# Normalising each head pair's output: eight one-column sums and transposes replaced by two full-width sums of squares

## The reference

```python
q = heads(jax.nn.silu(q_raw)) * (HGRN_KDIM ** -0.5)
v = heads(i_raw)
k_f, g_f = _hgrn2_forget(ffwd_raw, lb_fwd)
k_b, g_b = _hgrn2_forget(fbwd_raw, lb_bwd)
o_fwd = _gla_chunked(q, heads(k_f), v, heads(g_f))
o_bwd = flip(_gla_chunked(flip(q), flip(heads(k_b)), flip(v), flip(heads(g_b))))
o = (o_fwd + o_bwd).transpose(0, 2, 1, 3)
o = _rmsnorm(o, gnorm_w).reshape(b, s, HGRN_HEADS * HGRN_VDIM)
return o * jax.nn.silu(g_raw)
```

## Time and profile before

| what | value |
|---|---|
| median of 3 runs | 1879.22 us (1875.61 to 1879.58) |
| profiled execution's own time | 1879.22 us |
| its span in the profile | 1877.4 us |
| PE busy | 1680.7 us, 90% of the span |
| DVE, ACT, POOL busy | 780.7, 626.0, 551.4 us |
| mean granted PE clock | 0.948 of full speed |
| DMA | 123.5 MB, 66 GB/s on average |
| the head stage with attention, pairs 1 to 3 | about 123 to 478 us |
| the gates stage, with the attention of the fourth pair | about 478 to 683 us |

### The profile page before, as it was taken

One profiled execution on the slowest core, in us unless ns is written; L12 is line 12 of the kernel. 1 busy time (PEld: TensorE's weight loads), 2 busy tenths in 40 slices (PEclk: granted clock), 3 DMA queues, 4 the chain that ended last, 5 costly groups with the idle time before them and its releaser, 6 DMA issues.

```text
span 1877.4 us, 22957 instructions
## 1 busy us (share of the span) xinstructions
PE 1680.7 (90%) x9317; PEld 1308.7 (70%) x9317; DVE 780.7 (42%) x1229; ACT 626.0 (33%) x1011; POOL 551.4 (29%) x287
## 2 busy tenths in 40 slices
PE   5999999999689889999877999899996888999996
PEld 2788988889578667777646898555684665555564
DVE  3336365363765321111147611666514445444422
ACT  4322312313212321222332132666513224455632
POOL 2431213112433343333424222333423321010220
PEclk8999999899879989999888999899998889999998
DMA  4242212213123335343211112000011020000101
GB/s 135 92 145 68 90 45 67 89 35 99 50 63 90 90 112 179 112 134 123 90 45 45 63 57 68 18 18 18 1 59 45 23 72 17 17 18 23 45 23 45
DMA packets 128929, 123.50 MB, mean 66 GB/s; under 512 B 11252, under 2 KB 125040, under 8 KB 128848
## 3 DMA queue, kind: packets, MB, share of 16 engines
q1 hardware_dynamic: 128848, 122.37, 20.8%
HBM read 117.91 MB, written 2.10 MB: 64 GB/s over the span
## 4 chain that ended last, share of the span: by engine, by line
PE 63%; issue 13%; DVE 12%; POOL 7%; ACT 3%; DMA 2%; SPq 0%; DVEq 0%; POOLq 0%; ACTq 0%
PE ps L1801 5%; PE ps L1755 5%; PE ps L1756 5%; PE ps L1757 5%; POOL w_lo L982 4%; PE ps L2159 3%; PE ps L1959 3%; PE ps L2138 3%; PE ps L1960 3%; PE ps L1961 3%; PE ps L2148 3%; PE ps L1923 2%; PE ps L2025 2%; DMA raw<-in_w_in_dram 2%; PE ps L2016 2%
## 5 line engine op out<-in xcount | busy, mean ns | idle before, releaser
L982 POOL TENSOR_TENSOR w_lo<-raw,w_hi 128x2048 fp32r<-128x2048 f32 (+2 forms) x86 | 372.4, 4331 | 778.4 <-ACT w_hi L591 699.9
L1755 PE MATMUL ps<-h_hi,w_hi 128*128 128x512 f32 x656 | 274.1, 418 | 41.4 <-POOL h_lo L1042 14.0
L1756 PE MATMUL ps<-h_lo,w_hi 128*128 128x512 f32 x656 | 265.6, 405 | 0.0
L1757 PE MATMUL ps<-h_hi,w_lo 128*128 128x512 f32 x656 | 264.7, 404 | 0.0
L591 ACT ACTIVATE w_hi<-raw 128x2048 fp32r<-128x2048 f32 (+1 forms) x78 | 147.4, 1890 | 332.9 <-DMA raw<-in_w_in_dram 111.0
L1755 PEld LDWEIGHTS ps<-h_hi,w_hi 128*128 128x128 f32 x656 | 129.2, 197 | 82.2 <-issue 34.5
L1757 PEld LDWEIGHTS ps<-h_hi,w_lo 128*128 128x128 f32 x656 | 129.1, 197 | 29.1
L1756 PEld LDWEIGHTS ps<-h_lo,w_hi 128*128 128x128 f32 x656 | 129.4, 197 | 24.9
L1801 PE MATMUL ps<-qf,kf 128*128 128x64 f32 x448 | 91.0, 286 | 31.4 <-DVE tot_b L1241 27.8
L1801 PEld LDWEIGHTS ps<-qf,kf 128*128 128x128 f32 x448 | 73.2, 203 | 35.8 <-DVE tot_b L1241 29.9
L1801 PE MATMUL ps<-qb,kb 128*128 128x64 f32 x448 | 91.5, 288 | 0.0
(11 more groups left out here) (347 smaller groups left out, 3538.3 us busy)
## 6 DMA issues: line engine op xcount, KB each, us to landing
raw<-in_w_in_dram SPq DMA_DIRECT2D x32, 1024.0 KB
raw<-in_ada_w_dram SPq DMA_DIRECT2D x24, 1024.0 KB
raw<-in_a_w_in_dram SPq DMA_DIRECT2D x10, 1024.0 KB
raw<-in_w_in_dram SPq DMA_DIRECT2D x16, 512.0 KB
raw<-in_b_w_in_dram SPq DMA_DIRECT2D x5, 1024.0 KB
raw<-in_w_proj_a_dram SPq DMA_DIRECT2D x4, 1024.0 KB
raw<-in_w_proj_b_dram SPq DMA_DIRECT2D x4, 1024.0 KB
raw<-in_w_out_dram SPq DMA_DIRECT2D x4, 1024.0 KB
```

The lines of the kernel that those rows point to most:

```text
L982: nc.gpsimd.tensor_tensor(w_lo[:, ph.w(s), c], raw[:, s % 2, c], w_hi[:, ph.w(s), c].bitcast(F32), ALU.subtract).then_inc(s_lo, 1)
L1755: mm(ps[:, j, :], wh[:, k, c], xh[:, k, :], start=(k == 0), stop=False)
L1756: mm(ps[:, j, :], wh[:, k, c], xl[:, k, :], start=False, stop=False)
L1757: last = mm(ps[:, j, :], wl[:, k, c], xh[:, k, :], start=False, stop=(k == KT - 1))
```

## The change

The sums of squares are no longer taken per token on the partitions. Step 11 becomes two matmuls with a 128x128 matrix of ones as weights, one for each head, whose result [128, 512] holds each token's sum on every partition already. The scaling, the reciprocal and the root then work on the full [128, 1024] instead of [128, 8]; the copy that spread the root and step 12, the transposes, go away. `gla_out` goes away too: its two multiplications stand at the end of `gla_norm`, in slot 10, and the gate is kept in a tile of its own, `g_a`, instead of `y_a`. PE has 12 steps in place of 13, so all waits on `s_gla` are renumbered.

```diff
+        g_a = at("g_a", [P, 2, S], F32, r_s + 4 * KB)
...
-        g_ms = at("g_ms", [P, 2, 2 * NT], F32, region(64))
...
                 if tt == 10:
                     act.wait_ge(s_gms, g + 1)
-                    nc.scalar.activation(g_ms[:, 0, :], g_ms[:, 1, :], ACT.Sqrt).then_inc(s_grs, 1)
-                    act.wait_ge(s_grs, 2 * g + 1)
-                    nc.scalar.activation(qb[:, :, :].rearrange("p h (n c) -> p (h n) c", c=P),
-                                         g_ms[:, 0, :].unsqueeze(2).to_broadcast([P, 2 * NT, P]), ACT.Copy).then_inc(s_grs, 1)
+                    nc.scalar.activation(qb[:, :, :], kf[:, :, :], ACT.Sqrt).then_inc(s_grs, 1)
...
             def gla_norm(g):
-                dve.wait_ge(s_gla, 13 * g + 12)
-                v.tensor_scalar(g_ms[:, 0, :], ps[:, 4, 0:2 * NT], 1.0 / P, RMS_EPS, ALU.mult, ALU.add).then_inc(s_gcp_dve, 1)
+                dve.wait_ge(s_gla, 12 * g + 12)
+                v.tensor_scalar(kb[:, :, :], ps[:, 4:6, :], 1.0 / P, RMS_EPS, ALU.mult, ALU.add).then_inc(s_gcp_dve, 1)
                 dve.wait_ge(s_gcp_dve, 9 * g + 8)
-                v.reciprocal(g_ms[:, 1, :], g_ms[:, 0, :]).then_inc(s_gms, 1)
-
-            def gla_out(g):
-                dve.wait_ge(s_gla, 13 * g + 13)
-                gate = y_a[:, bass.ds(2 * g, 2), :]
-                v.scalar_tensor_tensor(kb[:, :, :], ps[:, 4:6, :], cols("gnorm_w"), gate, ALU.mult, ALU.mult).then_inc(s_gcp_dve, 1)
+                v.reciprocal(kf[:, :, :], kb[:, :, :]).then_inc(s_gms, 1)
+                dve.wait_ge(s_grs, g + 1)
+                v.scalar_tensor_tensor(kb[:, :, :], ps[:, 2:4, :], cols("gnorm_w"), qb[:, :, :],
+                                       ALU.mult, ALU.mult).then_inc(s_gcp_dve, 1)
                 dve.wait_ge(s_gcp_dve, 9 * g + 9)
-                v.tensor_tensor(gate, ps[:, 2:4, :], kb[:, :, :], ALU.mult).then_inc(s_y, 1)
+                v.tensor_tensor(y_a[:, bass.ds(2 * g, 2), :], kb[:, :, :], g_a[:, :, :], ALU.mult).then_inc(s_y, 1)
                 dve.wait_ge(s_y, g + 2)
...
                             if tt == 10:
                                 gla_norm(g)
-                            if tt == 11:
-                                gla_out(g)
...
-                            v.tensor_tensor(y_a[:, bass.ds(2 * it + j, 1), :], bank, a, ALU.mult).then_inc(s_free, 1)
+                            v.tensor_tensor(g_a[:, j, :], bank, a, ALU.mult).then_inc(s_free, 1)
...
-                elif step == 11:
+                else:
                     pe.wait_ge(s_osq, g + 1)
                     for h in range(2):
-                        for n in range(NT):
-                            last = mm(ps[:, 4, NT * h + n:NT * h + n + 1], qf[:, h, n * P:(n + 1) * P], ones[:, 0:1], start=True, stop=True)
-                else:
-                    pe.wait_ge(s_grs, 2 * g + 2)
-                    for h in range(2):
-                        for n in range(NT):
-                            last = nc.tensor.transpose(ps[:, 4 + h, n * P:(n + 1) * P], qb[:, h, n * P:(n + 1) * P], ident[:, :])
+                        last = mm(ps[:, 4 + h, :], ones[:, :], qf[:, h, :], start=True, stop=True)
                 last.then_inc(s_gla, 1)
```

More of the change, by code:

```diff
@@ L662, in gla_act @@
                     nc.scalar.activation(kb[:, :, :], kb_new[:, :, :], ACT.Copy).then_inc(s_kcopy, 1)
-                    act.wait_ge(s_gla, 13 * g + 1)
+                    act.wait_ge(s_gla, 12 * g + 1)
                     nc.scalar.activation(a_diag[:, :, :, :].rearrange("p h n s -> p (h n s)"),
@@ L666, in gla_act @@
                 if tt == 7:
-                    act.wait_ge(s_gla, 13 * g + 9)
+                    act.wait_ge(s_gla, 12 * g + 9)
                     nc.scalar.activation(a_128[:, :, :, :].rearrange("p h n s -> p (h n s)"),
@@ L670, in gla_act @@
                 if tt == 8:
-                    act.wait_ge(s_gla, 13 * g + 10)
+                    act.wait_ge(s_gla, 12 * g + 10)
                     nc.scalar.activation(a_256[:, :, :, :].rearrange("p h n s -> p (h n s)"),
@@ L674, in gla_act @@
                 if tt == 9:
-                    act.wait_ge(s_gla, 13 * g + 11)
+                    act.wait_ge(s_gla, 12 * g + 11)
                     nc.scalar.activation(qf[:, :, :], ps[:, 2:4, :], ACT.Square).then_inc(s_osq, 1)
@@ L1229, in gla_double @@
                     dve.wait_ge(s_gcp_act, 3 * g + 1)
-                dve.wait_ge(s_gla, 13 * g + l + 1)
+                dve.wait_ge(s_gla, 12 * g + l + 1)
                 if l > 1:
@@ L1277, in head_tiles @@
                                 gla_init(g)
-                                dve.wait_ge(s_gla, 13 * g + 1)
+                                dve.wait_ge(s_gla, 12 * g + 1)
                             if tt <= 7:
@@ L1283, in head_tiles @@
                             if tt == 8:
-                                dve.wait_ge(s_gla, 13 * g + 11)
+                                dve.wait_ge(s_gla, 12 * g + 11)
                             if tt == 10:
                                 gla_norm(g)
-                            if tt == 11:
-                                gla_out(g)
                         bank, a, b = ps[:, j, :], tmp[:, 2 * j, :], tmp[:, 2 * j + 1, :]
@@ L1855, in head_tiles @@
                                 gla(it - 1, 0)
-                            gla(it - 1, tt + 1)
+                            if tt <= 10:
+                                gla(it - 1, tt + 1)
                         if j == 0 and s in (4, 7):
@@ L1879, in _ @@
                         gla(PAIRS - 1, 0)
-                    if tt <= 11:
+                    if tt <= 10:
                         gla(PAIRS - 1, tt + 1)
```

## The result

| | before | changed |
|---|---|---|
| median (5 runs each) | 1878.70 us (1875.32 to 1879.58) | 1889.59 us (1886.45 to 1890.86) |
| ratio | 1 | 1.0063, 95% interval 1.0045 to 1.0082 |
| profiled execution, own time / span | 1879.22 / 1877.4 us | 1891.38 / 1889.5 us |
| PE, DVE busy | 1680.7, 780.7 us | 1677.2, 813.4 us |
| mean granted clock | 0.948 | 0.946 |

The changed kernel is 10.9 us slower by the medians; 10.1 was forecast (1889.3 us, range 1883 to 1898).

What follows compares the result with a forecast made beforehand. PE was taken to bound the head stage (busy 111.3 of 112.5 us), so its delays count. Terms 9.3 + 0.95 + 4.2 - 3.5 - 0.85 = +10.1 us on 1879.22 gave 1889.3 us, range 1883 to 1898.

Steps and rivals of the forecast that it cites:

- DVE's chain: At a pair's end, scaling through both products precedes the first `ga` tile's read-out; tile free after 12.4 us.
- Ends of pairs 1 and 2: Projection starts 5.9 us later, the 1.29 us wait for `qb` disappears; step 1 +4.65 us, twice, 9.3 us.
- End of pair 3: Step 0 waits for the output, 0.25 us later, and DVE has one more tile to read out: +0.95 us.
- Fourth pair: In the gates stage, DVE's longer chain delays the end of POOL's `w_lo`: +4.2 us.
- let it through in full: Fourth pair's `w_lo` delay counted whole, since SP's next load and PE's group 6 projection wait for it; bounds 0 and 5.
- The clock: Granted clock around the pair ends: -3.5 us for ends of pairs 1 and 2, -0.85 for the dip behind step 11.
- The dip behind step 11 of pair 2: Clock of 0.83 over ten us behind one-column matmuls, 1.7 us lost; half counted as regained, -0.85 us.
- 3 (POOL holds the reciprocal): POOL's `w_lo` makes the reciprocal wait, starting 3.4 us later at ends of pairs 1 to 3: +10.2, 1899.5 us; chance 0.03.
- 4 (a fast reciprocal): The wide reciprocal takes 1.22 us, like DVE's other operations: -5.6, 1873.6 us; chance 0.04.
- 5 (taken up later): Fourth pair's delay vanishes in the load waits and the clock gives all back: +1.75, 1881 us; chance 0.05.
- 1 (1897): PE's new idle costs 1.65 us twice and the old clock falls still come: +17.8, 1897 us; chance 0.12.
- 2 (1885.2): The clock gives all back, with no loss behind the idle time: +5.95, 1885.2 us; chance 0.16.

Runs made afterwards that it cites:

- e1: The changed kernel with DVE's reciprocal of 1024 columns cut to 8, so its output is not the reference's: 1866.97 us, ratio 0.9936.
- e6: The kernel before with only ACT's `w_hi` moved behind the copies of `kf` and `kb`: 1864.75 us, ratio 0.9939.
- e9: The changed kernel with reciprocal and root replaced by one ACT pass, an inverse square root: 1865.9 us, ratio 0.9945.
- e11: The kernel before with the wide normalisation for the fourth pair alone, in the gates stage: 1880.2 us, ratio 1.0031.
- e7: The changed kernel run and profiled once more, unaltered: 1887.63 us, ratio 1.0072.

## Why the prediction was right

Right in sign and size, and by its own steps; that the sum came within 1 us is in part luck, since chance falls of the clock move a profile by 3 us and two terms were mis-sized in opposite directions. Figures are from the first profile of the changed kernel.

- **DVE's chain.** Forecast: reciprocal 6.55, root 1.06, the projection 12.5 us after DVE's start, behind 6.9 us of idle. Measured: 6.55, 1.06, 12.46 (224.54 to 237.00), 6.61. The terms as listed, with 0.3 of hand-overs, add up to 12.55 to the free tile and not to the 12.4 that was written; the pauses turned out shorter, and the slip cost nothing. The line through 512 and 768 columns held at 1024, and `e1` shows that this term is the loss.
- **Ends of pairs 1 and 2.** Forecast: the delays without the clock are +9.3 us. Measured: over both cycles PE's time without work went from 4.9 to 15.6 us and its work at full clock from 225.0 (`e6`) to 223.5 (`e9`): +9.2. `qb` was indeed held up (5.63 us), and nobody waited for it.
- **End of pair 3.** +0.95 forecast, +0.9 measured to the next cut, where a single fall of the clock would be 3; step 1 came 0.7 later after DVE's start (15.53 against 14.82).
- **Fourth pair.** `w_lo` +4.2 later forecast, +4.2 measured (19.6 - 15.45); of it 3.65 us reach the merge. The step "let it through in full" was 0.55 too much.
- **The clock.** Forecast -4.35 us. Busy time of the two cycles above that of the same matmuls at full clock: before 236.6 - 225.0 = 11.6, changed 231.4 - 223.5 = 7.9. So -3.7 us. By term: the two falls behind step 1 went (-6.9; forecast -6.8), and `e6` shows that they hung on the 1.29 us of waiting. The restarts behind the idle time cost 2.0 and 2.7, not 1.65 each: +4.6 against +3.3. The dip behind step 11 of pair 2 went in full: -1.7 against -0.85, since its one-column matmuls are gone. Such a dip (0.67 over the 5.2 us behind DVE's scaling) stands at five of nine ends of pairs 1 to 3 in the three profiles with the old form there (before, `e6`, `e11`) and at none of 33 in the eleven with the wide form. These make -4.0; each of the two profiles also has one fall behind the wait for `tot_b`, which cancels. The second profile of the changed kernel (228.5) has none, and would give -6.6. That is beyond the 4.4 that the prediction had named as a sign of being wrong; by this account 3.2 of it are the fall that this profile happened not to have, and no part of the change.
- **The sum.** The terms as measured, 9.2 + 0.9 + 3.65 - 3.7, make 10.05; the medians say 10.9 and 11.9.
- **Rivals.** 3 (POOL holds the reciprocal): `w_lo` ran from 224.68 over the reciprocal, which took 6.55 us all the same. 4 (a fast reciprocal) fell with the 6.55 us. `e1` is about what it would have been: 1866.97, below the 1873.6 that I gave it, since I had left in the falls behind step 1. 5 (taken up later) fell by the gates stretch. 1 (1897) and 2 (1885.2) are the clock's two extremes. 2 is a ratio of 1.0032, below both intervals. 1 is 1.0095, above the first (to 1.0082) and inside the second (to 1.0098), so the times alone don't exclude it; the profiles do, as the old falls behind step 1, its premise, did not come.

What the prediction did not see is how dear the kernel before was at the same place. I counted the falling clock as something that the change might give back, but not that the wait alone made it, and so did not ask what a kernel without either wait would take. That was the larger thing to find: 11 us for moving one copy.

## What to carry to other kernels

Widening a small operation to save a transposition pays only where the wide one is cheap: price the reciprocal at 6.4 ns a column, not at the rate of its neighbours, and look at which tile's read-out stands behind it in the queue. An idle time of PE of a microsecond is to be priced with what the clock does behind it, above all in front of small matmuls. Before repairing a chain, run the version without its worst term: here one run showed that nothing else in the change cost anything. And run the old kernel without its own waits beside it: here that showed where most of the apparent gain came from.

## What the runs showed of the hardware

- A wait of PE between small matmuls can be followed by half clock, and need not be. Behind 0.86 us (for `tot_b`) the clock was 0.66 over ten us, a little over 3 us lost, in 10 of 42 cases; behind 1.07 to 1.76 us (for `qb`) in 6 of 10, among them both of 1.29 us in the profile of before. What decides between the two stays open.
- Ahead of a projection 0.64 to 0.82 us of idle cost nothing (`e9`, 5.57 us both times), 2.40 us nothing once and 1.6 once, 2.56 us 1.6 and 1.4, 6.61 us 2.0 and 2.7, and 2.2 and 2.8 in `e7`.
- Behind the one-column matmuls of step 11 the clock dipped in 5 of 9 cases, about 1.7 us lost each; behind the two wide ones in none of 33.
- DVE's operation on two SBUF tiles, started 0.9 us behind POOL's `w_lo`, took 5.53 us instead of 1.22 and ended 1.1 us after it; started before it, 1.22. The reciprocal, with one input, was not held.
- DVE's reciprocal is linear in columns: 3.353, 4.953 and 6.554 us for 512, 768 and 1024. ACT's root, logarithm, exponential and inverse root of 1024 columns all took 1.06 us, a table load 1.28.
